# The first three output tiles of the dense stages, skewed over three accumulation banks

## What is computed

```python
def s5_mixer(...):                      # layer 0: state-space scan, then
    g = gelu(y)
    out = g * sigmoid(g @ w_glu + b_glu)          # "glu": 1024 -> 1024
def conv_ffn(h, ...):                   # both layers
    up = h @ w_up                                 # "up": 1024 -> 2 * 2816
    a, g = split(causal_conv3(up) + conv_b)
    out = (silu(g) * a) @ w_down                  # "down": 2816 -> 1024
def shared_kv(x, ...):
    kv = modulate(rms_norm(x, norm_kv)) @ w_kv    # "kv": 1024 -> 1536
def nsa_mixer(h, ...):                  # layer 1: sparse attention
    q = h @ w_q                                   # "q": 1024 -> 1024
    return attention(q, kv rows, caches) @ w_o    # "o": 1024 -> 1024
# around every sub-layer:
x = x + gate * rms_norm(f(modulate(rms_norm(x), shift, scale)))
```

## Time and profile before

| | us |
|---|---|
| median of 3 runs | 1273.73 |
| lowest and highest | 1272.17, 1280.73 |
| profiled execution, its own time | 1273.41 |
| its span in the trace | 1271.7 |
| PE busy in the span | 1135.8 |
| DVE busy | 831.2 |
| ACT busy | 542.3 |
| POOL busy | 261.9 |

### The profile page before, as it was taken

One profiled execution on the slowest core, in us unless ns is written; L12 is line 12 of the kernel. 1 busy time (PEld: TensorE's weight loads), 2 busy tenths in 40 slices (PEclk: granted clock), 3 DMA queues, 4 the chain that ended last, 5 costly groups with the idle time before them and its releaser, 6 DMA issues.

```text
span 1271.7 us, 19251 instructions
## 1 busy us (share of the span) xinstructions
PE 1135.8 (89%) x6900; PEld 745.2 (59%) x6900; DVE 831.2 (65%) x1369; ACT 542.3 (43%) x1085; POOL 261.9 (21%) x384
## 2 busy tenths in 40 slices
PE   2599999988959999999699997999999599999995
PEld 0455566655626666666357665655665366666663
DVE  4689997998476787833664356566534667777434
ACT  2412111112446666643452415564444456666431
POOL 1185553770001111100100020003420012121000
PEclk8699998999869999999889877889999789999998
DMA  9769978656113434334312420005894114432431
GB/s 354 307 208 400 344 269 282 216 199 265 67 67 119 147 133 146 124 137 182 133 67 77 186 87 1 1 1 177 265 318 153 66 67 162 170 133 94 166 118 42
DMA packets 52530, 205.03 MB, mean 161 GB/s; under 512 B 7250, under 2 KB 36050, under 8 KB 41810
## 3 DMA queue, kind: packets, MB, share of 16 engines
q1 hardware_dynamic: 49362, 195.40, 42.1%
q0 software_dynamic: 3072, 8.39, 2.1%
HBM read 199.39 MB, written 4.38 MB: 160 GB/s over the span
## 4 chain that ended last, share of the span: by engine, by line
PE 76%; DVE 11%; ACT 4%; DMA 3%; SPq 3%; issue 3%; DVEq 0%; ACTq 0%; POOL 0%; POOLq 0%
PE PS L468 16%; PE PS L467 16%; PE PS L471 14%; PE PS L585 8%; PE PS L480 4%; DVE space L1304 3%; DVE wk_sb L1304 3%; PE PS L813 3%; PE PS L732 2%; PE PS L614 2%; PE PS L784 2%; PE PS L491 2%; PE PS L563 1%; PE PS L770 1%; DVE rinv L1308 1%
## 5 line engine op out<-in xcount | busy, mean ns | idle before, releaser
L467 PE MATMUL PS<-space_rounded 128*128 128x320 f32 x1344 | 572.1, 426 | 31.2 <-DVE space L1304 27.8
L468 PE MATMUL PS<-space_rounded,lo 128*128 128x320 bf16 x1344 | 430.4, 320 | 0.0
L471 PE MATMUL PS<-space,ring 128*128 128x320 bf16 x1344 | 405.3, 302 | 0.0
L1304 DVE TENSOR_TENSOR lo<-ring,space_rounded 128x1024 bf16<-128x1024 f32 (+1 forms) x172 | 205.9, 1200 | 250.9 <-ACT space_rounded L892 249.5
L467 PEld LDWEIGHTS PS<-space_rounded 128*128 128x128 f32 x1344 | 257.4, 192 | 105.6 <-DVE space L1304 40.7
L892 ACT ACTIVATE space_rounded<-ring 128x1024 fp32r<-128x1024 f32 (+1 forms) x172 | 177.1, 1033 | 264.3 <-PE PS L468 260.1
L468 PEld LDWEIGHTS PS<-space_rounded,lo 128*128 128x128 bf16 x1344 | 130.5, 97 | 128.8 <-issue 8.9
L471 PEld LDWEIGHTS PS<-space,ring 128*128 128x128 bf16 x1344 | 136.2, 101 | 0.0
L585 PE MATMUL PS<-space 128*128 128x256 f32 x512 | 115.4, 384 | 0.0
L585 PEld LDWEIGHTS PS<-space 128*128 128x128 f32 x512 | 96.4, 191 | 28.2 <-issue 15.6
L480 PE MATMUL PS<-ring,silc 128*32 128x512 f32 x448 | 66.8, 673 | 30.1 <-DMA ring<-w_mod 20.1
(11 more groups left out here) (197 smaller groups left out, 1455.4 us busy)
## 6 DMA issues: line engine op xcount, KB each, us to landing
ring<-w_mod SPq DMA_DIRECT2D x24, 2048.0 KB, 8.8
ring<-w_up SPq DMA_DIRECT2D x22, 2048.0 KB, 8.0
ring<-w_down SPq DMA_DIRECT2D x16, 1408.0 KB, 6.0
space<-pool_cmp SPq DMA_DIRECT2D x128, 128.0 KB, 2.8
ring<-w_mod_kv SPq DMA_DIRECT2D x4, 2048.0 KB, 10.4
ring<-w_kv SPq DMA_DIRECT2D x3, 2048.0 KB, 8.0
ring<-w_glu SPq DMA_DIRECT2D x2, 2048.0 KB, 10.5
ring<-w_q SPq DMA_DIRECT2D x2, 2048.0 KB, 12.7
```

The costliest lines, as they stand in the source:

```text
L467: pe.matmul(out, wr[:, p % SPLIT, at:at + P], xr[:, k, :], start=start, stop=False)
L468: mm = pe.matmul(out, lo[:, p % SPLIT, at:at + P], xh[:, k, :], start=False, stop=False)
L471: return pe.matmul(out, w, xl[:, k, :], start=False, stop=stop)
L1304: return dve.tensor_tensor(out, a, b, op)
```

## The change

The 8-step stages start with their first three output tiles together. At step s, TensorE runs feature tile s for output tile 0, feature tile s - 2 for output tile 1 and s - 4 for output tile 2, where these lie between 0 and 7: two steps with one product, two with two, four with three, two with two and two with one, 24 products as before. Each tile adds up in its own bank. Only tile 0's products wait for the splits. From tile 3 on, the order is the old one. It touches glu, kv, q and o through `dense`, and up of both layers through `ffn`; down has 22 steps and keeps its order.

```diff
--- before.py
+++ after.py
@@ -33,6 +33,7 @@
 NPJ = KVH * 2
 NMOD0 = 4
 SPLIT, PIECE = 3, 8
+SKEW = 2
 RING = 3
 SLOT = 4096
 ROUND = 12582912.0
@@ -500,8 +501,22 @@
 
 
                 m = 0
+                if kt == KT:
+                    for step in range(KT + 2 * SKEW):
+                        for i in range(3):
+                            k = step - SKEW * i
+                            if not 0 <= k < KT:
+                                continue
+                            if i == 0:
+                                pe.wait_ge(S(ready[0]), ready[1] + k + 1)
+                            mm = product(PS[:, banks[i], 0:T], chunks[0], KT * i + k, src, k, k == 0, k == KT - 1)
+                            if k == KT - 1:
+                                mm.then_inc(S(f"{tag}_mm"), 1)
                 for name in chunks:
                     for i in range(per):
+                        if kt == KT and m < 3:
+                            m += 1
+                            continue
                         if norm is not None and m >= 3:
                             sum_of(norm, m - 3)
                         if m >= len(banks):
@@ -521,13 +536,21 @@
 
             def ffn(l):
                 ready = split_of((2, 7)[l])
-                for j in range(FT):
+                for step in range(KT + 2 * SKEW):
+                    for i in range(3):
+                        k = step - SKEW * i
+                        if not 0 <= k < KT:
+                            continue
+                        if i == 0:
+                            pe.wait_ge(S(ready[0]), ready[1] + k + 1)
+                        mm = product(PS[:, i, 0:T], f"up{l}_0", KT * i + k, hb, k, k == 0, k == KT - 1)
+                        if i == 1 and k == KT - 1:
+                            mm.then_inc(S(f"up{l}_mm"), 1)
+                for j in range(1, FT):
                     if j >= 3:
                         pe.wait_ge(S(f"up_ev{l}"), 2 * (j - 2))
-                    for a in range(2):
+                    for a in range(1 if j == 1 else 0, 2):
                         for k in range(KT):
-                            if j == 0 and a == 0:
-                                pe.wait_ge(S(ready[0]), ready[1] + k + 1)
                             mm = product(PS[:, 2 * (j % 3) + a, 0:T], f"up{l}_{j // 2}", 16 * (j % 2) + KT * a + k, hb, k, k == 0, k == KT - 1)
                     mm.then_inc(S(f"up{l}_mm"), 1)
                 dense(f"down{l}", [f"down{l}_{j}" for j in range(8)], FT, U, 1, down_banks, f"down{l}_ev", (f"u_lo{l}", 0), norm=(3, 8)[l])
```

## The result

The changed kernel takes 1270.92 us (median of 20 runs, 1265.47 to 1275.43) against 1274.64 (20 runs, 1272.17 to 1281.62). The medians differ by 3.7 us. The ratio of the runs is 0.9959, 95% interval 0.9942 to 0.9976: about 5.2 us faster, with 3.1 to 7.4 possible. A second set of 12 runs (changed_again) beside 32 of the kernel before gave 0.9985 (0.9963 to 1.0006), 1.9 us, and that interval holds no change too. The forecast was +1.05 us, 1274.5. The measured time lies near the lower end of the stated 1270 to 1279, but the direction was wrong.

A forecast was written before the change was run, and what follows sets the result against it. It took TensorE's product lines (46% of the chain) as the bound, with time winnable where TensorE stands still or runs slow. Up -1.4, glu +3.0, o -0.65, kv 0, q +0.1 gave +1.05 on 1273.41: 1274.5 us, range 1270 to 1279.

The forecast's parts named there:

- Up: Start of up, both layers: filled gaps and an earlier clock rise win, -0.7 us each, -1.4 together.
- The 0.3 from filled gaps: Start of up: from the third product TensorE always has a second tile, worth 0.3 us without an earlier clock rise.
- My bound of 1.7: Start of up: the gain if the clock rises 3 us earlier, 1.7 us.
- Glu: Start of glu: the sum ahead of output tile 3 comes 1.85 us later, plus 1.1 for a clock fall: +3.0 us.
- The prediction's own sign of being wrong: In glu: the sum not later relative to the first product would show the forecast wrong.
- Piece 3: Weight piece ahead of output tile 3 in up, q and o: a pause of 0.1 us, at most 0.4 in up.
- O: Start of o: 0.77 us of gaps won, less 0.1 for piece 3: -0.65 us, bounds -0.8 and 0.
- Kv: Start of kv: output tile 3 still waits for piece 3, so 0; +2.2 us if the clock falls in the pause.
- Q: Start of q: no gap to fill, and piece 3 brings +0.1 us (0 to 0.4).
- Interleaved banks: Starts of stages: changing banks costs nothing; the rival has it keep the clock low in six heads, +35, 1308 us, chance 0.03.
- The first (the starts win, 1270.5): Rival: ACT's chain is shorter or the clock rises early; glu -0.6, up -1.6 twice, o -0.75; chance 0.18.
- The second, a clock that falls in glu's and kv's pauses: Rival: ahead of output tile 3 in glu and kv, 2.2 us each, +5.3 in all, 1278.7 us; chance 0.17.

The follow-up runs named there:

- changed_again: The changed kernel unaltered, measured again beside the kernel before: 1272.86 us (12 runs), ratio 0.9985 (0.9963 to 1.0006).
- two-bank: The changed kernel with only output tiles 0 and 1 skewed, two steps apart: 1269.85 us, one run.
- before_again: The kernel before the change, unaltered, profiled once more: 1275.93 us, one run.
- glu_pieces: The changed kernel with glu's weight pieces 1 and 2 made between the splits, sums left in place: 1267.34 us, one run.
- up_only: The changed kernel with the skewed order in up of both layers alone; glu, kv, q, o in the old order: 1271.72 us (12 runs), ratio 0.9970.
- skew_by_one: The changed kernel with output tiles 1 and 2 running one and two steps behind: 1277.39 us (10 runs), ratio 1.0005 (0.9975 to 1.0035).
- warm_changed: The changed kernel with 12 matmuls added in TensorE's idle time ahead of up (both layers) and kv: 1269.39 us, one run.
- warm_before: The kernel before with 12 matmuls added in TensorE's idle time ahead of up (both layers) and kv: 1276.47 us, one run.

## Why the prediction was wrong

Two steps failed: the point at which the clock rises in up, and the number of products that cover ACT's chain in glu. By the prediction's own steps, with means over the executions of the table with the order in question (without the warm ones, one-step and two-bank ones):

- **Up: the mis-sized term.** Foreseen -0.7 each. Measured 12.88 against 14.69 in layer 0 (seven and three executions) and 13.54 against 14.86 in layer 1: -1.8 and -1.3. The 0.3 from filled gaps was right: where the clock rose at nearly the same point (6.9 us in before_again, 7.0 in the changed kernel, both layer 1), the starts took 14.35 and 14.01. The failed step is when the clock rises. I carried glu's 4.6 us of low clock over to up, counted from the end of the gaps, and got a rise 1 us sooner. But in the old order, too, the gaps end before the splits do: its fifth product starts 4.5 us after the first, and the next three follow 0.8 apart. The skew ends the gaps at 2.2 us, 2.3 sooner. On average the clock rose 4.5 us after the first product against 7.7 in layer 0, and 5.8 against 8.1 in layer 1: 3.1 and 2.3 us sooner. At my own 0.47 per us, with the 0.3, that makes 1.8 and 1.4, close to the measured. Single rises vary by over 2 us. My bound of 1.7 was nearer than the value that I took, and layer 0 lies just outside it.
- **Glu: the failed step that turned the sign.** Foreseen +3.0, measured 18.93 against 18.73 (three and four executions), +0.2. Both waits were named rightly. But tile 0's last product is the 16th in the new order, not the 18th: steps 0 to 6 hold 1, 1, 2, 2, 3, 3, 3, and step 7 begins with tile 0. So eight products cover ACT's chain, not six, 0.9 us more. The chain itself took 5.35 us from the start of that product (323.54 to 328.89), 5.5 foreseen. The pause was 1.12 us and not 2.4, so the 1.1 us for a falling clock fell away too, and the clock had risen again by 320.46, 3.8 us after the restart, not 4.6. 0.9, 1.1 and 0.4 of the 2.8 us are so accounted for, and 0.15 by the chain; the rest is within the scatter of these starts. The prediction's own sign of being wrong was there: the sum came 18.44 to 18.58 us after the first product in the new order and 18.28 to 18.56 in the old, not clearly later.
- **Piece 3**, 0.1 us in up, q and o: nothing, by the same count (tile 1 ends with the 21st product, too, not the 22nd); with one step of skew it does appear (0.53 us).
- **O**: foreseen -0.65, measured 12.80 against 13.38, -0.6 on average. The mean hides two cases. Where four products ran at the low clock, the start took 13.22 before and 12.41 in glu_pieces, the 0.8 of the gaps. Where seven did, it took 13.71 in before_again and in the changed kernel alike. How many are low differs from execution to execution in either order.
- **Kv**: foreseen and measured 0, to 0.02 us.
- **Q**: foreseen +0.1, measured 12.36 against 12.71, but that is the clock: with four low products it took 12.08 in the old order (up_only) and 12.09 and 12.05 in the new (changed, glu_pieces).
- **Interleaved banks** cost nothing: in layer 0, from product 5 to 22, TensorE changes its bank 17 times in a row at 0.44 us a product. What the Trainium skill says of matmul groups cycling through PSUM banks (TensorE: Matmul & The Clock Gate, A second HAM failure mode: psum-queue depth-cycling) did not happen here; the clock rose sooner. That section tells of a clock that swings; starts that stay at the low clock throughout (1308) were its worst case. In all the new order changes its bank nineteen times in a row, not eighteen.
- **Idle time.** The 68.6 us and 37 waits at the head of the prediction count matmuls and weight loads together; the matmuls' own were 27.8 us in 6 waits. No term of the sum was taken from them.
- **The sum.** -3.1 + 0.2 + 0 - 0.35 - 0.6 = -3.9 us, inside both measured intervals; the -0.35 of q is no effect of the order. The forecast's own sum with up and glu put right (-3.1 and +0.2 for -1.4 and +3.0) would have been -3.5.
- **The rivals.** The first (the starts win, 1270.5) came nearest in time. Its early clock is what happened in up; glu's 0.6 was not won, and ACT's chain was only 0.15 shorter. The second, a clock that falls in glu's and kv's pauses, did not occur in the changed kernel: after 1.12 and 1.47 us idle it was high. Nor does the length of the pause decide alone, as it supposed. The clock fell at glu's 2.43 us in skew_by_one, and was high after kv's 2.69 in warm_changed.

Open: why attention comes out at 217 to 228 us with the same work. It goes with the clock, but what sets that in one execution, no run here shows.

## What to carry over

When products are fed by a slower producer, give TensorE a second output tile at once. In up the filled gaps themselves were worth 0.3 us and the earlier clock 1.0 to 1.5. Count in the new order which product frees a buffer or ends a tile, for everything behind it (pieces, take-outs, sums) has just that many products as cover. And where a wait for data turns into a wait for weights, moving the preparation of the weights wins more than the order did (here 6.8 and 8.5 us in the starts, on top of 3 to 5).

## What was not expected of the hardware

- A warm start does not hold: from the high level, products of 0.44 us every 1.1 us lost the clock by the fifth or sixth, and it took until the ninth or tenth to return (warm_before, in up and kv).
- The same pause can cost the clock or not: it was low after 2.43 us without a matmul (skew_by_one, glu) and high after 2.69 (warm_changed, kv).
- Identical instructions in attention took 217.48 to 227.87 us in 14 executions, at a granted clock of 0.90 to 0.85. The spans of one profile each can't carry a difference under 10 us here; the stage starts, which in one order repeat within 1.3 us, carry more.
